# A two-layer hybrid trunk on one core: the first norm's scaling moved two tiles ahead of its low parts, and the first parts of the index tiles moved around the modulation chunks

## The reference, cut to what matters

```python
cond = jax.nn.silu(c)
for i in range(DEPTH):
    mod = cond @ mod_w[i] + mod_b[i]
    sh1, sc1, g1, sh2, sc2, g2 = jnp.split(mod, 6, axis=-1)
    h = modulate(rms_norm(x, norm_mix_g[i]), sh1, sc1)      # h*(1+scale) + shift
    ...
        y = dsa_attention(h, attn_w_in[j], attn_w_out[j])   # begins with proj = h @ w_in
    ...
        y = s5_layer(h, ...)
    x = x + g1[:, None, :] * y
    h = modulate(rms_norm(x, norm_ffn_g[i]), sh2, sc2)
    x = x + g2[:, None, :] * conv_ffn(h, ...)
return rms_norm(x, final_g)
```

## Time and profile before

| | us |
|---|---|
| median of 3 runs | 762.85 (762.39 to 765.0) |
| the profiled execution: its own time | 762.1 |
| its span, first to last instruction | 760.1 |
| PE busy | 715.0 (94%) |
| DVE busy | 533.2 (70%) |
| ACT busy | 414.4 (55%) |

### The profile page before, as it was taken

How to read it: one execution, slowest core, us unless ns; L and a number is a source line. 1 busy time by engine, 2 the same in 40 slices (tenths; PEclk the granted TensorE clock), 3 DMA queues, 4 the chain that set the end, 5 groups by cost and what they waited for, 6 DMA issues and landing times.

```text
span 760.1 us, 18104 instructions
## 1 busy us (share of the span) xinstructions
PE 715.0 (94%) x7080; PEld 649.3 (85%) x7080; DVE 533.2 (70%) x897; ACT 414.4 (55%) x682; POOL 130.5 (17%) x120
## 2 busy tenths in 40 slices
PE   4789999999999999999999989789999999999996
PEld 1478999458798999999999789679979999999994
DVE  4766656995488778777867676756567666676665
ACT  4345644565465556675567654435556555555554
POOL 1000000211025343434303255520000000000000
PEclk9899999999999999999999999989999999999998
DMA  8989754796755766666676032009625555655521
GB/s 315 386 302 394 242 182 153 297 394 251 285 209 183 267 208 236 214 242 233 224 250 213 8 119 81 30 29 379 234 80 194 170 189 177 195 180 170 189 83 56
DMA packets 46072, 156.66 MB, mean 206 GB/s; under 512 B 6017, under 2 KB 7313, under 8 KB 46017
## 3 DMA queue, kind: packets, MB, share of 16 engines
q1 hardware_dynamic: 43344, 148.26, 56.1%
q10 hardware_dynamic: 2160, 6.38, 2.2%
q0 software_dynamic: 512, 1.25, 0.5%
HBM read 154.82 MB, written 1.05 MB: 205 GB/s over the span
## 4 chain that ended last, share of the span: by engine, by line
PE 80%; DVE 9%; issue 4%; ACT 3%; POOL 2%; DMA 1%; ACTq 0%; DVEq 0%; POOLq 0%
PE up L368 14%; PE up L370 13%; PE up L369 13%; PE acc L368 9%; PE acc L369 9%; PE acc L370 9%; PE gv L410 4%; DVE wlo L1168 2%; PE misc L469 1%; DVE tmp L1196 1%; DMA ident<-in_ident 1%; PE up L767 1%; ACT whi L822 1%; POOL arena L1777 1%; PE acc L499 1%
## 5 line engine op out<-in xcount | busy, mean ns | idle before, releaser
L1168 DVE TENSOR_TENSOR wlo<-raw,whi 128x1024 fp32r<-128x1024 f32 x188 | 253.3, 1361 | 75.5 <-ACT whi L822 70.5
L368 PE MATMUL up<-hh,whi 128*128 128x256 f32 x896 | 255.8, 286 | 2.2 <-DVE hl L1201 1.9
L370 PE MATMUL up<-hh,wlo 128*128 128x256 f32 x896 | 253.4, 283 | 0.0
L369 PE MATMUL up<-hl,whi 128*128 128x256 f32 x896 | 253.4, 283 | 0.0
L822 ACT ACTIVATE whi<-raw 128x1024 fp32r<-128x1024 f32 x185 | 192.6, 1052 | 40.8 <-PE acc L370 26.0
L368 PEld LDWEIGHTS up<-hh,whi 128*128 128x128 f32 x896 | 171.7, 192 | 10.5 <-issue 4.1
L369 PEld LDWEIGHTS up<-hl,whi 128*128 128x128 f32 x896 | 171.9, 192 | 0.0
L370 PEld LDWEIGHTS up<-hh,wlo 128*128 128x128 f32 x896 | 171.8, 192 | 0.0
L1499 DVE SCALAR_TENSOR_TENSOR ffn<-up,conv,ffn 128x254 f32<-128x254 f32 (+1 forms) x176 | 72.7, 475 | 45.6 <-ACT ffn L1017 45.3
L368 PE MATMUL acc<-ah,whi 128*128 128x256 f32 x352 | 99.8, 284 | 0.6 <-DVE wlo L1168 0.6
L369 PE MATMUL acc<-al,whi 128*128 128x256 f32 x352 | 99.6, 283 | 0.0
(11 more groups left out here) (240 smaller groups left out, 900.9 us busy)
## 6 DMA issues: line engine op xcount, KB each, us to landing
raw<-in_w SPq DMA_DIRECT2D x188, 512.0 KB, 3.6
mraw<-in_mw SPq DMA_DIRECT2D x48, 512.0 KB, 6.3
arena<-in_mw SPq DMA_DIRECT2D x24, 512.0 KB, 9.9
raw<-in_w SPq DMA_DIRECT2D x12, 256.0 KB, 12.5
tmp<-in_mw SPq DMA_DIRECT2D x6, 512.0 KB, 7.3
ffn<-in_mw SPq DMA_DIRECT2D x6, 512.0 KB, 8.3
tmp<-in_mw ACTq DMA_DIRECT2D x4, 512.0 KB, 6.7
ffn<-in_mw ACTq DMA_DIRECT2D x4, 512.0 KB, 9.1
```

Of the source, the lines that this page charges most:

```text
L368: pe.matmul(out, w_h, xh, start=first, stop=False, skip_group_check=skip)
L369: pe.matmul(out, w_h, xl, start=False, stop=False, skip_group_check=skip)
L370: return pe.matmul(out, w_l, xh, start=False, stop=last, skip_group_check=skip)
L1168: dve.tensor_tensor(wlo[:, n % SPL, :], raw[:, n % RAW, :], whi[:, n % SPL, :].bitcast(F32), ALU.subtract).then_inc(lo_ready, 1)
```

## The change

It rewrites the order of one stretch on two engines and adds or removes no arithmetic. On VectorE, in the first norm, the scaled tile is issued two tiles ahead of the low part for each set of four tiles. For `h` = 0 the low part of the first index slot comes ahead of `col_out`; for `h` = 1 it comes behind the second scaled tile. On PE `half(1, 0)` stands ahead of `gemv(2)`, `half(3, 0)` ahead of `gemv(3)`, and `half(4, 0)` ahead of `columns(1)`.

```diff
@@ -510,15 +510,15 @@
             gemv(1)
             columns(0)
             half(0, 0)
+            half(1, 0)
             pe.wait_ge(gm_ready, 1)
             gemv(2)
-            half(1, 0)
             half(2, 0)
+            half(3, 0)
             gemv(3)
-            half(3, 0)
+            half(4, 0)
             pe.wait_ge(hp_ready, 4)
             columns(1)
-            half(4, 0)
             half(5, 0)
             for n in range(RAW):
                 half(n, 1)
@@ -1324,14 +1324,18 @@
+                if h == 0:
+                    first_half(0, 0)
                 col_out(h)
                 first_scale(h)
                 first_scaled(4 * h)
-                first_half(0, h)
-                first_low(4 * h)
-                for k in range(4 * h + 1, 4 * h + 4):
-                    first_scaled(k)
+                first_scaled(4 * h + 1)
+                if h:
+                    first_half(0, 1)
+                for k in range(4 * h, 4 * h + 4):
                     first_low(k)
+                    if k < 4 * h + 2:
+                        first_scaled(k + 2)
                 for n in range(1, RAW):
                     first_half(n, h)
```

## The result

The changed kernel took 759.34 us in the median of 6 runs (757.83 to 761.32), the kernel before 763.73 us in 6 runs taken beside it (762.39 to 765.0). The ratio is 0.9944, with a 95% interval of 0.9928 to 0.9959: 4.3 us less, between 3.1 and 5.5. So it is faster, and by more than the 1.5 us that were forecast. One later run of the kernel before took 990.39 us, at a mean granted clock of 0.656; it is left out of every ratio and range here. The profiled execution took 759.71 us against 762.1, which is 2.4 us less; nearly half of the timed difference is thus not in the first pair of traces. The experiments go after both halves.

A forecast was written before the change was run, and what follows sets the result against it. PE held 80% of the chain, with two VectorE stretches of 5.48 us each on it. Terms -2.16, +2.16 +0.22 and -1.70 gave -1.48 us, so 761.4 us, with an 8 in 10 range of 759.2 to 763.2.

The forecast's parts named there:

- rival 1: No slow stretch at 25 us in the runs after: sum -3.75 us, 759.1 us; chance 0.12.
- `columns(1)` "not earlier" than 39.3: Sign in the profile after: `columns(1)` on PE at 39.3 us, where it started at 39.08 before.
- the three that were to show it wrong: `columns(1)` over 1 us before 39; clock 0.5 anywhere from 40 to 55; the 1.5 us at 45.7 gone by end.
- Step 1, tiles 0 to 3: VectorE's first four tiles: fourth low part 3.32 us after the first scaled tile instead of 5.48, 2.16 earlier.
- Step 2: PE up to `columns(1)`: the 2.16 us spent and 0.22 more, so `columns(1)` at 39.30 instead of 39.08.
- Step 3: Tiles 4 to 7: fourth low part at +3.78 us instead of +5.48, -1.70; `half(1, 1)` at 45.69 instead of 47.17.
- I cost the rest at nothing: Behind `half(1, 1)`: no cost; a late load or copy would take back at most the 1.48 us.
- Rival 2: The clock falls a second time at about 45 us: +1.9 us, 764.8 us; chance 0.07.
- Rival 3: PE's work from 45.7 us on meets something unmoved, above all a load: gain 0, 762.85 us; chance 0.15.

The follow-up runs named there:

- before, first: First trace of the kernel before, no edit; the profiled execution took 762.1 us.
- before, second: The kernel before traced again, no edit; 762.53 us.
- before, third: The kernel before traced a third time, no edit; 761.43 us.
- VectorE's order alone: VectorE as in the changed kernel, PE's order as in the kernel before; 759.01 us, ratio to before 0.9937.
- PE's order alone: PE as in the changed kernel, VectorE's order as in the kernel before; 765.97 us, ratio to before 1.0029.
- full-array fillers: Added matmuls of 128x128 weights on a 128x256 tile; 2 + 6 around `columns(0)` in the changed kernel: 760.16 us, ratio to before 0.9955.

## Why the prediction was right in direction and too small

The forecast was 761.4 us with a range of 8 in 10 of 759.2 to 763.2; the median of 759.34 lies 0.14 us inside its low end. That is luck more than insight: it is outside the forecast's own range (760.5 to 762.1), and the low end stood where it did because of rival 1, which did not occur. The chances were wrong too: 0.75 went to a time within 0.3% of before, 0.22 to a faster one, and the faster one came. Of the signs that were named, `columns(1)` "not earlier" than 39.3 failed (38.58), and with it the starts behind it came early; none of the three that were to show it wrong came about.

A view used for this: VectorE's reciprocal (L1193) stands once in each norm, so its starts cut an execution into stages. In us, from the traces:

| trace | norm 0 to 1 | norm 1 to 2 | norm 2 to 3 | norm 3 to 4 |
|---|---|---|---|---|
| before, first | 192.1 | 214.0 | 133.4 | 198.6 |
| before, second | 193.6 | 214.0 | 132.8 | 198.6 |
| before, third | 192.8 | 214.0 | 132.8 | 198.6 |
| changed | 190.6 | 214.0 | 132.6 | 198.6 |
| VectorE's order alone | 188.4 | 214.0 | 134.4 | 198.6 |
| PE's order alone | 196.2 | 214.0 | 134.0 | 198.7 |

- **Step 1, tiles 0 to 3, was right.** Forecast 3.32 us from the first scaled tile to the fourth low part, measured 3.37. The weight's low part ahead of `col_out` cost nothing: `col_out` follows the start of `columns(0)` by 1.21 us, before by 1.19.
- **Step 2 is where the sum went wrong.** It took the rise of the clock at 32.0 "as before". The matmuls of `half(1, 0)` were 0.21 apart as forecast, but the clock rose at 29.9, and chunk 2 took 1.83 us instead of 2.72. `columns(1)` came 16.98 behind `columns(0)`; the forecast was 39.30 - 21.18 = 18.12. These 1.14 us are the largest error of the sum: 0.89 is chunk 2, the rest `half(1, 0)`, which ended earlier. The step treated the low stretch as fixed to the program. It is not: without full-array fillers around `columns(0)` it began anywhere from 22.5 to 25.5 us, and, what I had not weighed at all, its length goes with VectorE's order, 10.2 us before against 6.8 after for stretches that begin before 24 us.
- **Step 3 was right.** Forecast 3.78, measured 3.62; `half(1, 1)` 6.23 us behind `columns(1)` against 6.39 forecast, and PE's wait there 0.99 against 1.2.
- **"I cost the rest at nothing" holds in part.** Counted from `columns(0)`, the first pair of traces is 2.8 us apart at `half(1, 1)` (1.48 forecast), 2.1 at norm 1 and 2.8 at the end. In absolute times it is 2.4 at the end, because `columns(0)` itself came 0.4 later in the changed kernel's trace (21.60 against 21.18), ahead of everything that the change moves. Of these, 0.8 lie in the state-space layer, where the first trace of before had a low stretch of 3.4 us at 445 and the changed kernel's has none. Between chunk 4 and norm 1 the three traces of before themselves differ by 0.7 us, so what was given back between (0.7) can't be pinned down.
- **The timed 4.3 against the profiled 2.4.** The three profiled executions of before (762.1, 762.5, 761.4) all lie below the medians of its series (763.2 to 764.0), while the changed kernel's (759.71) lies near its median. The mean granted clock of the runs is 0.983 for before and 0.988 for the changed kernel. At equal clock the two are about 2 us apart, though only one run of the changed kernel stands at each: at 0.984 before has a mean of 763.4 (23 runs, up to 765.7) and the changed kernel 761.3, at 0.986 762.6 (14 runs) and 760.7, at 0.988 762.2 (2 runs) and 759.7. The rest goes with the clock: the 24 runs of before at 0.980 and 0.981 took 763.1 to 766.3, and the changed kernel has three runs at 0.990 and 0.991, with 757.8 to 759.0. That runs with a lower clock are longer is shown; in which stage those slowest runs of before lose it is open, since none of them left a trace.
- **The rivals.** Rival 1 (no slow stretch) gave the right size, -3.75, by a mechanism that did not occur: the stretch stayed and became shorter. Where it was taken away with full-array fillers, `columns(1)` came 15.83 behind `columns(0)`, which is what this rival's sum says (37.03 - 21.18 = 15.85), so its arithmetic for the start holds; the time gained nothing. The prediction allowed for executions in which the stretch is absent; it was absent in none of the nine traces of the table. Rival 2, a second fall at 45, does exist, but in the kernel before and with PE's order alone (46.6 to 47.4), and in no trace with the new VectorE order. Rival 3, given back later, did not happen beyond 0.7 us.
- **PE's half of the change** is a loss by itself (2.2 us slower alone). The sum of step 2 contains it, one index half more ahead of `columns(1)`, but nets it against the 2.16 us of step 1 and never asks what VectorE's part would be worth without it: by the traces 1.3 us more at `half(1, 1)`.

## What to carry to other kernels

Where two engines hand tiles to each other in a fixed order, issue the producer's next tile before waiting for the consumer's answer: here the step fell from 1.45 to 0.8 us a tile. Then ask what else stands ahead of the instruction that starts the next such chain: moving independent work in front of it cost about its full length (1.3 us for an index half of 1.4). A forecast should not pin a low-clock stretch of one trace to its place; take two or three traces of the kernel before, compare them from an instruction ahead of the change, and allow for the change itself to move or shorten the stretch.

## What was not expected of the hardware

- The place and length of the low-clock stretch vary between executions of one program: 22.66 to 32.90 and 25.00 to 31.82 us in two traces of before. The Trainium skill says in "TensorE: Matmul & The Clock Gate", Part 1, that the number of slow matmuls at a kernel's start differs from run to run; these traces agree, with a stretch further in that began from 22.5 to 25.5 us and lasted 3.4 to 10.2. That the length goes with VectorE's order is what the table above shows.
- Ten one-row matmuls of zeros, back to back, did not keep the clock up in the kernel before (PE busy 4.19 of 5.00 us from 20 to 25, clock 0.85 and then 0.50). Six full-array ones, with two more ahead of `columns(0)`, did hold it there in every trace that has them (5.00 of 5.00, clock 1.00), though in the kernel before it fell later, at 29.84. The two differ in the kind of matmul and in the gap ahead of `columns(0)`, so which of these counted is open.
- A low-clock stretch that begins at 441 to 450 us, in the state-space layer, is in seven of the fourteen traces. From norm 2 to norm 3 the kernels take 132.5 to 132.8 us without it, 133.4 to 134.4 with one of 3.4 us and 135.7 with one of 6.8: as much as most edits at the start are worth.
